# Attention of a two-layer block: when VectorE makes each output's low part, and when it evacuates the first group of an expansion

## Chip, cores and metric

The kernel runs on one core of one Trainium2 chip. The metric is the device time of one execution in microseconds (us), taken as the median of several runs. The engines are TensorE (PE, matmuls), VectorE (DVE), ScalarE (ACT), GpSimd (POOL) and SyncE (SP, which issues the DMAs).

## What is computed

Two transformer-like blocks one after the other, batch 1, 256 positions, model width 1024, all in float32. What matters here are the two attention parts with the projections around them:

```python
# first block: 8 heads of 128; one block of 256 keys, so plain causal attention
p = jax.nn.softmax(jnp.concatenate([s_sel, s_own], axis=-1), axis=-1)
yb = einsum(p_own, v_own)
merged = gates[:, :, 0] * (ya @ w_proj_rnn) + gates[:, :, 1] * (yb @ w_proj_attn)
# second block: 8 sliding-window heads with a sink, then 8 MLA heads
o_a = swa_sink_attention(qa, ka, va, swa_sinks)
q   = (cq @ w_uq);  kvb = ckv @ w_ukv        # the expansions of the latents
o_b = mla_attention(q_nope, q_rope, k_nope, k_rope, vb)
y = sigmoid(g_a) * (o_a @ w_o_swa) + sigmoid(g_b) * (o_b @ w_o_mla)
x = x + y @ w_out
```

The two blocks also have a recurrent branch, RMS norms and feed-forward parts, which the change does not touch.

## The kernel before

**Precision by parts.** Every large product is made of three matmuls on float32r parts: a number is split into a high part (a copy rounded by ScalarE, `whi`, `ahi`) and a low part (the remainder, `number - high`, made by VectorE, `wlo`, `alo`). So every weight tile is read twice before PE may use it.

**Slabs.** The weights come in slabs of 128 x 2048 numbers through a ring of three buffers. For each slab SP loads `raw`, ScalarE makes `whi` (function `hi`, L490, called through `pre`), VectorE makes `wlo` (`lo`, L856, called through `pre`), and PE multiplies. `pre(s + 2)` means that both engines convert the slab that PE uses two slabs later.

**Hand-written order.** Each engine has its own program, written out by hand, loop by loop over the slabs; the only links between engines are semaphores. An engine goes through its own list in that order, and what stands in a list behind a waiting instruction waits too.

**Attention units and steps.** Attention is cut into 24 units: 0 to 7 are the heads of the first block, 8 to 15 the sliding-window heads and 16 to 23 the MLA heads of the second. Each unit goes through a pipeline whose stages are one step apart (`LAG_S` 1, `LAG_E` 2, `LAG_N` 3, `LAG_PT` 4, `LAG_PV` 5), and one call `att(step)` in each engine's program does the engine's share of all stages of that step. In one step PE transposes q and k of a new unit (L1489), multiplies scores of the previous one (L1501, L1502), transposes the probabilities of an older one (L1512) and multiplies the oldest by its values (L1526, L1528; called PV here, and PV(u) for unit u). ScalarE then evacuates: transposes, probabilities (L536), the high part of the PV output (L541), and makes the exponentials (L553). VectorE scales the probabilities (L896 to L898), masks scores and takes maxima (L904 to L915), and makes the **low part** of the PV output (L920), called lo(u) here.

**One PSUM buffer for PV.** `PSPV` is a single bank. lo(u) is the last reader of the output of unit u, and PE asks for it before it overwrites the bank with the next unit (L1518): PV(u) waits for the semaphore `att lo` (`aL`) to count u, which means lo(u-1) has been made. Nothing in PE's list behind PV(u), the matmuls of the slab included, can start before.

**Where the steps stand.** The first block's steps 0 to 12 stand one to a slab: eight gate slabs (G0 to G7 here), four slabs of `w_proj_rnn` (P0 to P3) and the first of `w_proj_attn` (A0). PV(0) is in G5, PV(3) in P0 and PV(7) in A0. The second block's steps 100 to 120 go by `STEPS_AT`: one step each in the slabs of the expansions UQ0, UQ1 and UKV (PV(8), PV(9), PV(10)), two steps each (called A and B here) in GB0 to GB3 and OSWA0, OSWA1 (PV(11) to PV(22)), one in OMLA0 (PV(23)). PE does step A at the start of a slab and step B in its middle (in GB0 a little later).

VectorE's list for such a slab s reads (L1227 to L1260):

```python
for step in steps[:1]: att(step)        # A
pre(s + 2)                              # wlo, behind ScalarE's whi
for step in steps[1:]: att(step)        # B
gate(s, ...)   # or branch(...): evacuation of slab s, needs its last matmul
```

and for one-step slabs `att`, `pre(s + 2)`, then `gate` or `branch`. In UQ0 to UKV `pre(s + 2)` stands at the end of the slab instead (`late_cut`), on ScalarE too. In P3 a second `pre`, that of slab P3 + 3, follows behind `branch` (the `cut()` of L1092). ScalarE's list has `att(A)`, the `whi` of slab s + 2, `att(B)`.

UKV is the slab of `w_ukv`; its four groups of matmuls use two banks in turn. VectorE evacuates groups 0 and 2 (`kv_evac`, L1224), ScalarE groups 1 and 3. PE's group 2 needs the bank of group 0.

Of the kernel before, what the change touches and what calls it, by code (L numbers as in the profile page):

```python
# [17 lines left out]
SEQ = 256  # L18
# [5 lines left out]
HEADS = 8  # L24
# [125 lines left out]
LAG_S, LAG_E, LAG_N, LAG_PT, LAG_PV = 1, 2, 3, 4, 5  # L150


def steps_at(s):

    if S_GATE <= s < S_PR + LAG_PV:
        return [s - S_GATE]
    if S2_GA <= s <= S2_OMLA:
        first = sum(STEPS_AT[:s - S2_GA])
        return [100 + first + i for i in range(STEPS_AT[s - S2_GA])]
    return []  # L160
# [7 lines left out]
def early_att(s):  # L168

    return S_GATE < s < S_PA or S2_GA < s < S2_OUT  # L170


def late_cut(s):

    return S2_UQ <= s <= S2_UKV


def gate_of(s):

    if S2_GA <= s < S2_UQ:  # L180
        return s - S2_GA
    if S2_GB <= s < S2_OSWA:
        return s - S2_GB + S2_UQ - S2_GA
    return None


def unit_of(step):

    if 0 <= step < HEADS:
        return step  # L190
    if 100 <= step < 100 + 2 * HEADS:
        return step - 100 + HEADS
    return None


def program(nc, t):
    f32, f32r = mybir.dt.float32, mybir.dt.float32r
    ALU, ACT, AX = mybir.AluOpType, mybir.ActivationFunctionType, mybir.AxisListType.X
    with ExitStack() as ctx:
        def sb(name, shape, dt=f32):  # L200
            return ctx.enter_context(nc.sbuf_tensor(name, shape, dt))

        def sem(name):
            return ctx.enter_context(nc.semaphore(name))
# [5 lines left out]
        pairs = [(sb(f"ahi{i}", [P, KD, SEQ], f32r), sb(f"alo{i}", [P, KD, SEQ], f32r)) for i in range(2)]  # L210
# [91 lines left out]
        PST, PSS, PSPT, PSPV, PSA, PSB = ps[2], (ps[3], ps[7]), (ps[4], ps[6]), ps[5], ps[6], ps[7]  # L302

        def sums_banks(n):
# [24 lines left out]
        aT, aTe, aS, aM, aE, aN, aPT, aPTe, aPV, aH, aL = (sem(n) for n in (  # L329
            "att_T", "att_T_out", "att_S", "att_max", "att_exp", "att_norm", "att_PT", "att_PT_out",  # L330
            "att_PV", "yb_hi", "yb_lo"))
# [513 lines left out]
        def _(e):  # L845
            count = [0]

            def link(ins):

                count[0] += 1  # L850
                ins.then_inc(dve_step, 1)
                e.wait_ge(dve_step, count[0])
# [6 lines left out]
            def pre(s):  # L859
                if s < SLABS:  # L860
                    lo(s, s % RING)
# [26 lines left out]
            def att(step):  # L888
                kind_base = 0 if step < 100 else 100
                u, un, ul = (unit_of(step - lag) if step - lag >= kind_base else None  # L890
                             for lag in (LAG_S, LAG_N, LAG_PV))
                if un is not None:
                    e.wait_ge(aE, un + 1)
                    if 8 <= un < 16:
                        link(e.tensor_tensor(sums[:, un % 3, :], sums[:, un % 3, :], esink[:, un % 3, :], ALU.add))
                    link(e.reciprocal(rinv[:, un % 2, :], sums[:, un % 3, :]))  # L896
                    e.tensor_scalar(pr[:, un % 3, 0:P], pr[:, un % 3, 0:P], rinv[:, un % 2, 0:1], None, ALU.mult)
                    e.tensor_scalar(pr[:, un % 3, P:3 * P], pr[:, un % 3, P:3 * P], rinv[:, un % 2, 1:2], None,  # L898
                                    ALU.mult).then_inc(aN, 1)
                if u is not None:  # L900
                    e.wait_ge(aS, u + 1)
                    if u >= 2:
                        e.wait_ge(aE, u - 1)
                    link(e.tensor_tensor(sm[:, u % 2, :], PSS[u % 2][:, 0:3 * P],  # L904
                                         masks[:, 1 if 8 <= u < 16 else 0, :], ALU.add))
                    e.reduce_max(mx[:, u % 2, 0:1], sm[:, u % 2, 0:P], AX)
                    link(e.reduce_max(mx[:, u % 2, 1:2], sm[:, u % 2, P:3 * P], AX))
                    if u < 8:
                        e.tensor_tensor(nb[:, u % 3, :], mx[:, u % 2, :], cq[:, 1, :, u], ALU.mult).then_inc(aM, 1)
                    elif u < 16:  # L910
                        hd = swa_head(u)
                        e.tensor_scalar(nb[:, u % 3, :], mx[:, u % 2, :], -(64 ** -0.5), sinks[:, 1, hd:hd + 1],
                                        ALU.mult, ALU.min).then_inc(aM, 1)
                    else:
                        e.tensor_scalar(nb[:, u % 3, :], mx[:, u % 2, :], -(MLA_D ** -0.5), None,  # L915
                                        ALU.mult).then_inc(aM, 1)
                if ul is not None:
                    e.wait_ge(aH, ul + 1)
                    rows, chunk = yb_place(ul)
                    e.tensor_tensor(pairs[2][1][rows, chunk, :], PSPV[rows, 0:SEQ],  # L920
                                    pairs[2][0][rows, chunk, :].bitcast(f32), ALU.subtract).then_inc(aL, 1)


            e.memset(epst[:, :], EPS)
            for b in range(2):
# [112 lines left out]
            def gate(s, i):  # L1038
                normed(GROUP_OF[(s, 0)], gate_tile(i))

            def branch(g, tiles, dst):

                e.wait_ge(group_done, g + 1)
                e.scalar_tensor_tensor(dst[:, tiles, :], dst[:, tiles, :], 1.0,
                                       ps[BANK[g]][:, :].rearrange("p (m n) -> p m n", m=2),
                                       ALU.add, ALU.mult).then_inc(bank_free["dve"], 1)
                e.wait_ge(bank_free["dve"], emptied(g)[1])
# [171 lines left out]
            def kv_evac(i):  # L1219

                g = GROUP_OF[(S2_UKV, i)]
                e.wait_ge(group_done, g + 1)
                for dst, src in kv_parts(ps[BANK[g]], i // 2, 0):
                    ins = e.tensor_copy(dst, src)  # L1224
                ins.then_inc(bank_free["dve"], 1)

            for s in range(S2_GA, FFN2):  # L1227
                steps = steps_at(s)
                if s == S2_UKV:
                    kv_evac(0)  # L1230
                for step in steps[:1]:
                    att(step)
                if early_att(s) and not late_cut(s) and s < S2_OUT - 1:
                    pre(s + 2)
                for step in steps[1:]:
                    att(step)
                if S2_OSWA <= s < S2_OMLA:
                    e.wait_ge(gate_t, 12)
                    c = 4 * (s - S2_OSWA)
                    branch(GROUP_OF[(s, 0)], slice(c, c + 2), T0)  # L1240
                if s == S2_GA + 1:
                    cq_parts(0)
                    cq_parts(1)
                if s == S2_GA + 2:
                    cq_parts(2)
                if gate_of(s) is not None:
                    gate(s, gate_of(s))
                if s == S2_UKV:
                    kv_evac(2)
                if S2_UQ <= s <= S2_UKV:  # L1250
                    pre(s + 2)
                if S2_OSWA <= s < S2_OMLA:
                    c = 4 * (s - S2_OSWA) + 2
                    branch(GROUP_OF[(s, 1)], slice(c, c + 2), T0)
                if S2_OMLA <= s < S2_OUT:
                    e.wait_ge(gate_t, 16)
                    for i in range(2):
                        c = 2 * (s - S2_OMLA) + i
                        branch(GROUP_OF[(s, i)], slice(2 * c, 2 * c + 2), T1)
                        merge(c, 4, (lambda: pre(s + 2)) if s == S2_OUT - 1 and i == 0 else nothing)  # L1260
                if S2_OUT <= s < FFN2:
                    i = s - S2_OUT
                    residual(s, i)
                    if s < FFN2 - 1:
                        pre(s + 3)
                    norm_lo(3, pcol[:, FFNG:FFNG + KD], pairs[2][1], pairs[2][0], (2 * i, 2 * i + 1))
                if s in (S2_OUT - 1, FFN2 - 1):
                    pre(s + 3)
# [455 lines left out]
def swa_head(u):  # L1724

    return (u - 8) // 2 + 4 * ((u - 8) % 2)


def yb_place(u):

    if u < 8:
        return slice(0, P), u
    b = u % 2
    return slice(64 * b, 64 * b + 64), (u - 8) // 2
# [47 lines left out]
```

## Time and profile before

| | |
|---|---|
| median of 3 runs | 825.85 us (825.42 to 826.04) |
| the profiled execution's own time | 825.37 us |
| its span, first to last instruction | 823.5 us |
| PE busy with matmuls | 798.3 us, 97% |
| VectorE busy | 599.6 us, 73% |
| ScalarE busy | 457.7 us, 56% |
| granted TensorE clock, mean | 0.998 |

Busy is the time in which an engine executes; the rest it waits, or has run out of work. The 1.9 us between span and time lie outside the instructions. Of PE's idle time 11.7 us is the start, before the first weights are split.

### The profile page before, as it was taken

The numbers are of one execution on the slowest core, as the hardware profiler recorded it, in microseconds if no ns is written. First come the engines' busy times: TensorE is split into PE (matmuls) and PEld (weight loads), VectorE is DVE, ScalarE is ACT, GpSimd is POOL, SyncE is SP. The second block draws the span as 40 slices with busy tenths as digits, with TensorE's granted clock in tenths as the row PEclk, the third lists the DMA queues.
The fourth block names the chain that finished last, engine by engine and source line by source line (L and its number), as shares of the span: only waits on it lengthen the run. The fifth ranks groups of instructions, "written<-read, shape, count | busy, mean of one in ns | idle before, by whom it ended". The sixth has DMA issues, their size and how long they took to land.

```text
span 823.5 us, 13642 instructions
## 1 busy us (share of the span) xinstructions
PE 798.3 (97%) x5240; PEld 729.5 (89%) x5240; DVE 599.6 (73%) x773; ACT 457.7 (56%) x611; POOL 83.9 (10%) x94
## 2 busy tenths in 40 slices
PE   4999999999999999999999999999999999999996
PEld 4998888999999899999998899889999888888884
DVE  5895798666667898777787868777777856766653
ACT  5669855566335555444444667667556544454443
POOL 2030142000021100000000440500013000000000
PEclk9999999999999999999999999999999999999999
DMA  9997899776878789788886895564669978888841
GB/s 227 218 214 162 189 197 200 159 153 134 174 175 184 156 184 214 166 196 197 179 190 144 183 196 130 106 152 103 134 138 215 202 175 188 197 184 187 193 102 51
DMA packets 112781, 140.99 MB, mean 171 GB/s; under 512 B 5474, under 2 KB 95586, under 8 KB 112738
## 3 DMA queue, kind: packets, MB, share of 16 engines
q1 hardware_dynamic: 112594, 140.30, 78.6%
q8 instruction: 29, 0.48, 0.3%
q14 instruction: 14, 0.11, 0.1%
q10 hardware_dynamic: 144, 0.10, 0.0%
HBM read 139.33 MB, written 1.05 MB: 170 GB/s over the span
## 4 chain that ended last, share of the span: by engine, by line
PE 79%; DVE 10%; ACT 6%; issue 2%; POOL 1%; DMA 1%; SPq 0%; DVEq 0%; ACTq 0%; POOLq 0%
PE pp L1418 20%; PE pp L1377 15%; PE pp L1379 15%; PE pp L1378 15%; PE pp L1420 10%; DVE wlo L856 4%; ACT whi L490 1%; PE pp L1526 1%; POOL vv L1289 1%; PE pp L1502 1%; PE pp L1489 1%; PE pp L1512 1%; DMA raw<-in_w_in 1%; ACT gate L610 1%; PE pp L1501 1%
## 5 line engine op out<-in xcount | busy, mean ns | idle before, releaser
L856 DVE TENSOR_TENSOR wlo<-raw,whi 128x2048 fp32r<-128x2048 f32 x131 | 302.9, 2314 | 123.1 <-ACT whi L490 123.1
L490 ACT ACTIVATE whi<-raw 128x2048 fp32r<-128x2048 f32 x131 | 250.1, 1911 | 98.6 <-PE pp L1379 79.8
L1377 PE MATMUL pp<-ahi,whi 128*128 128x256 f32 x768 | 221.5, 288 | 13.8 <-DVE alo L871 11.7
L1418 PE MATMUL pp<-ahilo,whi 128*128 128x512 f32 x704 | 221.4, 396 | 0.0
L1378 PE MATMUL pp<-alo,whi 128*128 128x256 f32 x768 | 218.5, 284 | 0.0
L1379 PE MATMUL pp<-ahi,wlo 128*128 128x256 f32 x768 | 218.4, 284 | 0.0
L1377 PEld LDWEIGHTS pp<-ahi,whi 128*128 128x128 f32 x768 | 148.5, 193 | 15.5 <-DVE wlo L932 11.7
L1420 PEld LDWEIGHTS pp<-ahilo,wlo 128*128 128x128 f32 x704 | 132.2, 188 | 31.2
L1378 PEld LDWEIGHTS pp<-alo,whi 128*128 128x128 f32 x768 | 148.7, 194 | 0.1
L1379 PEld LDWEIGHTS pp<-ahi,wlo 128*128 128x128 f32 x768 | 148.5, 193 | 0.0
L1420 PE MATMUL pp<-ahilo,wlo 128*128 128x256 f32 x704 | 138.3, 278 | 0.0
L1418 PEld LDWEIGHTS pp<-ahilo,whi 128*128 128x128 f32 x704 | 108.0, 189 | 0.8
L1377 PE MATMUL pp<-whi,ahi 128*128 128x512 f32 (+2 forms) x252 | 97.9, 389 | 1.1 <-DVE alo L1150 1.1
L1379 PE MATMUL pp<-whi,alo 128*128 128x512 f32 (+2 forms) x252 | 96.9, 384 | 0.0
L1378 PE MATMUL pp<-wlo,ahi 128*128 128x512 f32 (+2 forms) x252 | 96.9, 384 | 0.0
L715 ACT ACTIVATE qk<-pp 128x512 f32<-128x512 f32 x44 | 26.3, 598 | 120.0 <-PE pp L1420 120.0
L1108 DVE TENSOR_TENSOR qk<-pp,qk 128x512 f32<-128x512 f32 x44 | 30.4, 690 | 40.9 <-ACT qk L715 40.8
L1377 PEld LDWEIGHTS pp<-whi,ahi 128*128 128x128 f32 x252 | 47.3, 188 | 10.6 <-issue 1.4
L1379 PEld LDWEIGHTS pp<-whi,alo 128*128 128x128 f32 x252 | 47.3, 188 | 9.0
L1378 PEld LDWEIGHTS pp<-wlo,ahi 128*128 128x128 f32 x252 | 47.4, 188 | 8.2
L1289 POOL TENSOR_TENSOR vv<-vv 128x512 f32<-128x512 f32 x12 | 24.1, 2006 | 252.0 <-ACT vv L507 251.5
L1377 PE MATMUL pp<-ahilo,whi 128*128 128x256 f32 x128 | 36.7, 287 | 0.0
(200 smaller groups left out, 847.9 us busy)
## 6 DMA issues: line engine op xcount, KB each, us to landing
raw<-in_w_in SPq DMA_DIRECT2D x80, 512.0 KB, 6.7
raw<-in_w_up SPq DMA_DIRECT2D x44, 512.0 KB, 6.3
raw<-in_w_gate SPq DMA_DIRECT2D x44, 512.0 KB, 6.3
raw<-in_w_down SPq DMA_DIRECT2D x44, 512.0 KB, 6.5
raw<-in_w_out SPq DMA_DIRECT2D x16, 512.0 KB, 6.3
raw<-in_w_proj_rnn SPq DMA_DIRECT2D x8, 512.0 KB, 6.0
raw<-in_w_proj_attn SPq DMA_DIRECT2D x8, 512.0 KB, 6.0
raw<-in_w_o_swa SPq DMA_DIRECT2D x4, 512.0 KB, 5.9
```

The lines of the kernel that those rows point to most:

```text
L490: e.activation(whi[slot][:, :], raw[slot][:, :], ACT.Copy).then_inc(hi_ready, 1)
L610: ins = e.activation(dst, ps[BANK[g]][:, SEQ * m:SEQ * m + SEQ], ACT.Tanh, scale=0.5, bias=halfb[:, 8 * (i // 4) + blk:8 * (i // 4) + blk ...
L715: e.activation(dst, banks[:, :, SEQ:2 * SEQ], ACT.Copy).then_inc(f_cross, 1)
L856: e.tensor_tensor(wlo[slot][:, :], raw[slot][:, :], whi[slot][:, :].bitcast(f32), ALU.subtract).then_inc(lo_ready, 1)
L1108: return e.tensor_tensor(dst, banks[:, :, 0:SEQ], dst, ALU.add)
L1289: e.tensor_tensor(SQ[:, 0:2, :], SQ[:, 0:2, :], SQ[:, 2 * i:2 * i + 2, :], ALU.add).then_inc(folded, 1)
L1377: e.matmul(out, lhs[0], rhs[0], start=first, stop=False, skip_group_check=True)
L1378: e.matmul(out, lhs[0], rhs[1], start=False, stop=False, skip_group_check=True)
L1379: return e.matmul(out, lhs[1], rhs[0], start=False, stop=last, skip_group_check=True)
L1418: e.matmul(out[:, m, :], w[m][0], ACT2[:, k, :], start=k == 0, stop=False, skip_group_check=True)
L1420: ins = e.matmul(out[:, m, 0:SEQ], w[m][1], ACT2[:, k, 0:SEQ], start=False, stop=k == KD - 1, skip_group_check=True)
L1489: ins = e.transpose(PST[0:d, SEQ * i + P * h:SEQ * i + P * h + P], src, ident[:, :])
```

## The change

VectorE's `att(step)` no longer ends with lo(u) of its own PV unit. It begins with the low part of the unit whose PV was in the step before (`unit_of(step - LAG_PV - 1)`). Only the last unit of each block (7 and 23), which has no next step, keeps its low part at the end of its own step. Beside that, `kv_evac(0)` in slab UKV moves from before VectorE's step 107 to behind it. No instruction is added or removed; the lists of PE, ScalarE, GpSimd and SyncE stay as they are.

```diff
--- before.py
+++ after.py
@@ -889,6 +889,9 @@
                 kind_base = 0 if step < 100 else 100
                 u, un, ul = (unit_of(step - lag) if step - lag >= kind_base else None
                              for lag in (LAG_S, LAG_N, LAG_PV))
+                before = unit_of(step - LAG_PV - 1) if step - LAG_PV - 1 >= kind_base else None
+                if before is not None:
+                    out_lo(before)
                 if un is not None:
                     e.wait_ge(aE, un + 1)
                     if 8 <= un < 16:
@@ -914,12 +917,15 @@
                     else:
                         e.tensor_scalar(nb[:, u % 3, :], mx[:, u % 2, :], -(MLA_D ** -0.5), None,
                                         ALU.mult).then_inc(aM, 1)
-                if ul is not None:
-                    e.wait_ge(aH, ul + 1)
-                    rows, chunk = yb_place(ul)
-                    e.tensor_tensor(pairs[2][1][rows, chunk, :], PSPV[rows, 0:SEQ],
-                                    pairs[2][0][rows, chunk, :].bitcast(f32), ALU.subtract).then_inc(aL, 1)
-
+                if ul is not None and ul in (7, 8 + 2 * HEADS - 1):
+                    out_lo(ul)
+
+            def out_lo(u):
+
+                e.wait_ge(aH, u + 1)
+                rows, chunk = yb_place(u)
+                e.tensor_tensor(pairs[2][1][rows, chunk, :], PSPV[rows, 0:SEQ],
+                                pairs[2][0][rows, chunk, :].bitcast(f32), ALU.subtract).then_inc(aL, 1)
 
             e.memset(epst[:, :], EPS)
             for b in range(2):
@@ -1226,10 +1232,10 @@
 
             for s in range(S2_GA, FFN2):
                 steps = steps_at(s)
+                for step in steps[:1]:
+                    att(step)
                 if s == S2_UKV:
                     kv_evac(0)
-                for step in steps[:1]:
-                    att(step)
                 if early_att(s) and not late_cut(s) and s < S2_OUT - 1:
                     pre(s + 2)
                 for step in steps[1:]:
```

**Place 1: VectorE in a slab with two steps (GB2, MLA units).** The rows before run from the low part of step A to the low part of step B and the gate (`gate<-pp`) behind it; L920 is the low part, L856 the `wlo` of the slab two ahead.

```order
L920 TENSOR_TENSOR ahilo<-pp,ahilo 64x256
L856 TENSOR_TENSOR wlo<-raw,whi 128x2048
L896 RECIPROCAL rinv<-sums 128x2
L897 TENSOR_SCALAR pr<-pr,rinv 128x128
L898 TENSOR_SCALAR pr<-pr,rinv 128x256
L904 TENSOR_TENSOR sm<-pp,masks 128x384
L906 TENSOR_REDUCE mx<-sm 128x1
L907 TENSOR_REDUCE mx<-sm 128x1
L915 TENSOR_SCALAR nb<-mx 128x2
L920 TENSOR_TENSOR ahilo<-pp,ahilo 64x256
L885 TENSOR_TENSOR gate<-pp,rstd_bc 128x512
```

The same stretch of the changed program, where L927 is the low part:

```order
L856 TENSOR_TENSOR wlo<-raw,whi 128x2048
L927 TENSOR_TENSOR ahilo<-pp,ahilo 64x256
L899 RECIPROCAL rinv<-sums 128x2
L900 TENSOR_SCALAR pr<-pr,rinv 128x128
L901 TENSOR_SCALAR pr<-pr,rinv 128x256
L907 TENSOR_TENSOR sm<-pp,masks 128x384
L909 TENSOR_REDUCE mx<-sm 128x1
L910 TENSOR_REDUCE mx<-sm 128x1
L918 TENSOR_SCALAR nb<-mx 128x2
L885 TENSOR_TENSOR gate<-pp,rstd_bc 128x512
L927 TENSOR_TENSOR ahilo<-pp,ahilo 64x256
```

The low part of step A stood ahead of `wlo` and stands behind it; that of step B stood ahead of the gate and stands behind it.

**Place 2: VectorE from slab P2 to slab A0 of the first block.** L1044 (L1050 in the changed program) is `branch`, the evacuation of a slab. Before:

```order
L856 TENSOR_TENSOR wlo<-raw,whi 128x2048
L1044 SCALAR_TENSOR_TENSOR gate<-gate,pp 128x512
L920 TENSOR_TENSOR ahilo<-pp,ahilo 128x256
L856 TENSOR_TENSOR wlo<-raw,whi 128x2048
L1044 SCALAR_TENSOR_TENSOR gate<-gate,pp 128x512
L856 TENSOR_TENSOR wlo<-raw,whi 128x2048
L920 TENSOR_TENSOR ahilo<-pp,ahilo 128x256
L1044 SCALAR_TENSOR_TENSOR gate<-gate,pp 128x512
```

And now:

```order
L856 TENSOR_TENSOR wlo<-raw,whi 128x2048
L1050 SCALAR_TENSOR_TENSOR gate<-gate,pp 128x512
L927 TENSOR_TENSOR ahilo<-pp,ahilo 128x256
L856 TENSOR_TENSOR wlo<-raw,whi 128x2048
L1050 SCALAR_TENSOR_TENSOR gate<-gate,pp 128x512
L856 TENSOR_TENSOR wlo<-raw,whi 128x2048
L927 TENSOR_TENSOR ahilo<-pp,ahilo 128x256 x2
L1050 SCALAR_TENSOR_TENSOR gate<-gate,pp 128x512
```

The low part of unit 6 was in front of two `wlo` and a `branch`; it is now behind them, next to that of unit 7.

**Place 3: VectorE from the end of slab UQ1 to GB0.** L1224 (L1230 in the changed program) is `kv_evac`, two copies for each group. Before:

```order
L920 TENSOR_TENSOR ahilo<-pp,ahilo 64x256
L856 TENSOR_TENSOR wlo<-raw,whi 128x2048
L1224 COPY gg<-pp 128x4x64
L1224 COPY qk<-pp 128x256
L895 TENSOR_TENSOR sums<-sums,esink 128x2
...
L912 TENSOR_SCALAR nb<-mx,sinks 128x2
L920 TENSOR_TENSOR ahilo<-pp,ahilo 64x256
L1224 COPY gg<-pp 128x4x64
L1224 COPY qk<-pp 128x256
L856 TENSOR_TENSOR wlo<-raw,whi 128x2048
```

And now:

```order
L856 TENSOR_TENSOR wlo<-raw,whi 128x2048
L927 TENSOR_TENSOR ahilo<-pp,ahilo 64x256
L898 TENSOR_TENSOR sums<-sums,esink 128x2
...
L915 TENSOR_SCALAR nb<-mx,sinks 128x2
L1230 COPY gg<-pp 128x4x64
L1230 COPY qk<-pp 128x256
L1230 COPY gg<-pp 128x4x64
L1230 COPY qk<-pp 128x256
L856 TENSOR_TENSOR wlo<-raw,whi 128x2048
L927 TENSOR_TENSOR ahilo<-pp,ahilo 64x256
```

The first two copies moved behind the step's arithmetic, and both low parts moved behind the `wlo` that followed them.

## Rows read from the trace of the kernel before

**Rows 1.** The page, busy time of PE over the whole span
```profile
PE 798.3 (97%) x5240; PEld 729.5 (89%) x5240; DVE 599.6 (73%) x773; ACT 457.7 (56%) x611; POOL 83.9 (10%) x94
```

**Rows 2.** Who PE waited for, whole span: us, times, longest
```profile
PE pp L1526 <- DVE ahilo L920: 1.2, 2, 0.7
...
PE pp L1377 <- DVE qk L1224: 0.4, 1, 0.4
```

**Rows 3.** Timeline, UKV: start us, us, engine, instruction, [idle before it]
```profile
530.24 0.43 DVE L920 TENSOR_TENSOR ahilo<-pp,ahilo 64x256 fp32r<-64x256 f32 x1
...
530.82 0.67 PE L1526 MATMUL pp<-pT,qk 128*128 128x256 f32 x2 [0.46 <-DVE ahilo L920]
```

**Rows 4.** Timeline, slab OSWA0, PE, ACT and DVE
```profile
578.69 0.39 PE L1501 MATMUL pp<-qkT 96*128 96x128 f32 x2
...
579.68 0.60 PE L1526 MATMUL pp<-pT,qk 128*128 128x256 f32 x2
...
581.62 0.43 DVE L920 TENSOR_TENSOR ahilo<-pp,ahilo 64x256 fp32r<-64x256 f32 x1
581.83 1.90 ACT L490 ACTIVATE whi<-raw 128x2048 fp32r<-128x2048 f32 x1
...
583.53 0.60 PE L1526 MATMUL pp<-pT,qk 128*128 128x256 f32 x2
583.76 2.29 DVE L856 TENSOR_TENSOR wlo<-raw,whi 128x2048 fp32r<-128x2048 f32 x1 [1.71 <-ACT whi L490]
...
585.97 0.16 DVE L896 RECIPROCAL rinv<-sums 128x2 f32<-128x2 f32 x1
```

**Rows 5.** Timeline, slab GB2
```profile
560.31 0.60 PE L1526 MATMUL pp<-pT,qk 128*128 128x256 f32 x2
...
565.27 0.60 PE L1526 MATMUL pp<-pT,qk 128*128 128x256 f32 x2
...
566.60 0.16 DVE L896 RECIPROCAL rinv<-sums 128x2 f32<-128x2 f32 x1
```

**Rows 6.** Timeline, slabs UQ0 to UKV
```profile
524.65 0.60 PE L1526 MATMUL pp<-pT,qk 128*128 128x256 f32 x2
...
525.41 2.43 DVE L856 TENSOR_TENSOR wlo<-raw,whi 128x2048 fp32r<-128x2048 f32 x1 [4.22 <-ACT whi L490]
...
531.10 2.44 DVE L856 TENSOR_TENSOR wlo<-raw,whi 128x2048 fp32r<-128x2048 f32 x1 [0.43 <-ACT whi L490]
```

**Rows 7.** Timeline, slab GB0
```profile
541.02 0.60 PE L1526 MATMUL pp<-pT,qk 128*128 128x256 f32 x2
...
542.13 0.15 DVE L895 TENSOR_TENSOR sums<-sums,esink 128x2 f32<-128x2 f32 x1
...
545.25 0.60 PE L1526 MATMUL pp<-pT,qk 128*128 128x256 f32 x2
...
547.50 0.15 DVE L895 TENSOR_TENSOR sums<-sums,esink 128x2 f32<-128x2 f32 x1
```

**Rows 8.** Timeline, start of slab P3 (w_proj_rnn)
```profile
214.98 0.49 PE L1512 MATMUL pp<-ident,pr 128*128 128x128 f32 x3
...
215.25 0.69 DVE L1044 SCALAR_TENSOR_TENSOR gate<-gate,pp 128x512 f32<-128x512 f32 x1 [1.31 <-PE pp L1379]
215.30 0.60 PE L1526 MATMUL pp<-pT,vv 128*128 128x256 f32 x2
```

**Rows 9.** Timeline, start of slab A0 (w_proj_attn)
```profile
221.71 0.60 PE L1526 MATMUL pp<-pT,vv 128*128 128x256 f32 x2
...
226.19 0.42 DVE L920 TENSOR_TENSOR ahilo<-pp,ahilo 128x256 fp32r<-128x256 f32 x1
```

**Rows 10.** Stretches: busy by engine (instructions), granted PE clock, DMA, GB/s
```profile
12.00:18.00 6.00, 6.00 (x30) 6.00 (x30) 5.97 (x11) 5.74 (x10) 2.84 (x3) 1.00 1.12 222
170.00:226.00 56.00, 56.00 (x455) 55.19 (x454) 36.38 (x58) 29.75 (x53) 0.00 (x0) 1.00 0.69 150
817.00:821.00 4.00, 0.00 (x0) 0.00 (x0) 3.15 (x6) 2.07 (x7) 0.00 (x0) 0.87 0.35 131
```


## The prediction

> **What bounds the kernel now.** I read the page first, then PE's waits, then the timeline of both attention parts. The page has PE busy for 97% of the span [rows 1], so what matters is whether the change adds to PE's waits or takes some away. There is little to take: over the whole span PE waited 1.2 us for a low part, twice, and 0.4 us for the evacuation of the expansion [rows 2]. VectorE and ScalarE look idle a third of the time, but in the attention they are on a leash: `wlo` starts when `whi` ends, `whi` starts when ScalarE has done step A, and step A contains the evacuation of PV(A). What the reader is to see in the rows of slab OSWA0 [rows 4] is how close behind PE that loop runs.
>
> **The price list.** Where PE was caught waiting for a low part, PV started 530.82 - 530.24 = 0.58 us after the low part's start [rows 3]. I use 0.57 throughout. After such a wait PE loses about 0.07 us more (PV's pair takes 0.67 instead of 0.60 us [rows 3, 4]).
>
> **Step B of the two-step slabs.** PV(B) needs lo(A). Before, lo(A) stood ahead of `wlo`; in OSWA0 it began at 581.62, and PV(B) at 583.53 found it done 1.5 us earlier [rows 4]. Now it stands behind `wlo` (place 1). `whi` runs from 581.83 to 583.73, `wlo` from 583.76, and the instruction behind it begins at 585.97 [rows 4]. That is where lo(A) goes, so PV(B) starts at 585.97 + 0.57 = 586.54, 3.0 us late. Can `wlo` come earlier? No: `whi` follows PV(A) by 2.15 us and all of that is ScalarE's step A, so the loop moves with PE and the loss comes back in each slab. The same sum for the others:
> - GB2: 566.60 + 0.57 - 565.27 = 1.9 us [rows 5]. GB1 and GB3 have the same pattern at 1.9 us each, so 5.7 in all.
> - GB0: 547.50 + 0.57 - 545.25 = 2.8 us [rows 7].
> - OSWA0: 3.0 us. OSWA1 has less arithmetic in its step; between the 1.9 of GB2 and the 3.0 of OSWA0 I take 2.1.
>
> Together 13.6 us.
>
> **The one-step slabs of the expansions.** `wlo` stands at the end of the slab here, and the low part behind it.
> - PV(9) needs lo(8), which goes behind the `wlo` of 525.41. That one takes 2.43 us, and the next instruction overlaps its end by some 0.08, so 527.76 + 0.57 = 528.33 against 524.65: 3.7 us [rows 6].
> - PV(10) needs lo(9), behind the `wlo` of 531.10. If nothing had moved: 531.10 + 2.36 + 0.57 = 534.03, against an arrival of 530.82 - 0.46 = 530.36 [rows 3, 6], 3.7 us. PE's arrival and `whi`, which waits for UQ1's last group, both move by the 3.7 us of PV(9); ScalarE gains back some 0.2 us of backlog (an estimate). I take 3.5, and 3.0 net of the old wait of 0.46.
> - PV(11) needs lo(10), behind the `wlo` that ends before 542.13: 542.13 + 0.57 - 541.02 = 1.7 us [rows 7]. In this slab two small waits for `kv_evac` fall away (next part), 0.4 us each; the first moves PE and `whi` together, the second only PE, which makes the wait 2.0 and the net loss 1.3.
> - PV(13) had the wait of 0.7 us [rows 2]; its lo(12) has only the gate in front of it now, and PE comes to it later by all the waits above, so it is in time (next part): -0.7.
>
> Together 7.3 us.
>
> **Behind the evacuation of a slab.** Ahead of PV(1) to PV(6) and of PV(13), (15), (17), (19), (21) and (23) the low part goes behind `gate` or `branch`, which needs the last matmul of the slab before. `branch` begins 0.27 us after PE's first instruction of the new slab (215.25 - 214.98 [rows 8]), takes 0.69 and waits for its own end (0.72, an estimate), then 0.57: PV may start 1.56 us into the slab. In P3 it started at 0.32 [rows 8], so 1.2 us each for PV(4), PV(5), PV(6) and PV(21), 4.9 us, and 1.5 us for PV(23), which is PE's first instruction. `gate` has no wait for its own end, and the next instruction overlaps it by some 0.08 as behind `wlo` (585.97 against 583.76 + 2.29 [rows 4]): 0.60 us, 1.44 in all. With scores but no transposes ahead PV comes at 0.99 us (579.68 - 578.69 [rows 4]), 0.45 each for PV(3) and PV(19); with transposes, four instructions more, it comes at about 1.4, and I cost PV(2), (13), (15) and (17) at nothing. What covers them is just that arithmetic of PE; were it gone, each would cost 1.1. PV(1) finds VectorE 0.6 us behind: 0.6. Together 7.9 us. VectorE's own step starts 0.4 us later everywhere; behind it stands only scaling and masking, which waits for ScalarE's `whi` afterwards in any case.
>
> **Unit 6, the worst one.** PV(7) in A0 needs lo(6). Before, that was made in P3's step. Now it stands behind `wlo`, `branch`, and the second `wlo` (place 2), in the place where lo(7) began at 226.19: 226.19 + 0.57 - 221.71 = 5.05 us [rows 9].
>
> **`kv_evac(0)`.** It moves behind step 107, some 2.1 us. Had PE not been held up, that would be 2 us on PE's group 2. But PV(10) stands ahead of group 0 and now waits, so VectorE has finished its step (2.5 us behind the start of lo(9)) when group 0 ends, and the evacuation of 0.75 us ends before PE wants group 2, about 3.2 us behind PV(10). Cost nothing; this cover is PE's own new wait. The two old waits go, 0.4 us as in [rows 2], and as much, an estimate, for GB0's first group, which waits for the other evacuation.
>
> **The sum.** 13.6 + 7.3 + 7.9 + 5.05 = 33.9 us, and 15 restarts of 0.07 us make 1.0: 34.9 us. PE has no slack to give it back. Against the profiled execution's 825.37 us that is 860.3; the median of the runs lies 0.5 us above it, so I predict 860.5 us.
>
> **TensorE's clock.** At the start of the program PE does 30 matmuls in 6 us, where the attention stretch has 455 in 56 us, 49 in 6 [rows 10]. The granted clock reads 1.00 in both, but the spacing of the first is that of the lower of the two levels, 1.2 GHz. The slow spell cost some 19 / 8.1 = 2.3 us. Near the end, in 4 us without a matmul, the mean granted clock is 0.87 [rows 10], so it fell to the lower level in the last microsecond of them. The new wait before PV(7) is longer than that, those before PV(9) and PV(10) about as long.
>
> The Trainium skill says the same (TensorE: Matmul & The Clock Gate, "HAM oscillation — how this bites in real kernels"): an idle gap puts the clock back to its lower level, and the next stretch of work starts slow. By that rule the sum would be three such spells longer; the gap at the end agrees, and no gap inside this kernel was long enough to show it.
>
> **Rivals.**
> - *The clock falls at all three long waits*: 860.5 + 3 x 2.3 = 867.4 us. For it: the fall near the end. Against it: two of the three waits are only as long as the gap after which the row shows the fall. One fall, at PV(7), gives 862.8 and counts to the forecast.
> - *The loop doesn't move with PE*: once PE is late, `whi` and `wlo` run on ahead, only the first wait of each kind is paid. Then about half, 17 us: 843. For it: ScalarE is busy 56%. Against it: `whi` begins right behind ScalarE's step A [rows 4].
> - *Faster*: VectorE is held up by lo(u) waiting for ScalarE's high part, and the change frees it. The three known waits of PE, 0.46, 0.7 and 0.4 us, go: 825.85 - 1.6 = 824.2 us. That needs lo(A) done by the time of PV(B), which is to say 585.97 + 0.57 before 583.53; it misses by 3 us.
> - *No change*: if the two orders made VectorE reach lo(A) at the same time as before. In every two-step slab a whole `wlo` of 2.3 us lies between the places.
>
> **How the numbers follow.** Forecast, 853 to 865 us: 0.66. Clock, 865 to 872: 0.12. The loop catches up, 835 to 853: 0.16. Faster 0.03, no change 0.01, beyond these 0.02. The range that leaves out no more than two in ten reaches into both neighbours: 848 to 868. A difference of 0.2% or less is about what a measurement of this kernel can't tell from none. Faster 0.03, same 0.01, slower 0.96.
>
> **What the changed profile would show.** Right: PE's waits for L927 about 15 to 18 times, 35 us together; the longest, 5 us, at the first `w_proj_attn` slab; in each two-step slab PV(B) 0.57 us behind the start of a low part that stands directly behind `wlo`; no wait for `kv_evac`. PE's busy share falls to 93%. Wrong in size: two-step slabs whose PV(B) waits less than 1 us (the loop caught up), or slow matmuls behind PV(7). Wrong altogether: PE's waits for the low part at 2 us or less.

## The result and the profile after

The changed kernel takes 872.43 us (median of 4 runs, 871.56 to 876.26), the kernel before 825.63 us in the same session: a ratio of 1.0575, 95% interval 1.0555 to 1.0595, 46.8 us more. The profiled execution took 871.61 us, its span is 869.8 us and its mean granted TensorE clock 0.980 where it was 0.998. The prediction was 860.5 us in a range of 848 to 868, so the direction and the waits were right and the time lies above the range.

The page of the changed kernel, PE's busy time and the granted clock in 40 slices of the span (tenths, 9 is 90% or more):

```profile
PE 813.7 (94%) x5240; PEld 741.5 (85%) x5240; DVE 600.4 (69%) x773; ACT 457.5 (53%) x611; POOL 81.8 (9%) x94
...
PEclk9999999999999999999999998799899999999999
```

With the same 5240 matmuls PE is busy for 15.4 us longer than in [rows 1], which waits alone can't do (a restart behind each adds some 0.07 us, 1.3 us in all). That is the first sign of something beside waits: matmuls that got slower. Slices 25, 26 and 29 of the span (522 to 565 and 609 to 631 us), in the second block's attention, show where it is most.

PE's waits, total us, times, longest:

```profile
PE pp L1532 <- DVE ahilo L927: 33.0, 18, 4.9
```

Against 1.2 us in [rows 2]: 31.8 us more, in 18 places. PE no longer waits for the evacuation of the expansion.

The timeline of the changed kernel at A0, UQ1, UKV and OSWA0 (start, us, engine, instruction, idle before it); L927 is the low part, L1532 PV:

```profile
228.64 2.29 DVE L856 TENSOR_TENSOR wlo<-raw,whi 128x2048 fp32r<-128x2048 f32 x1 [1.31 <-ACT whi L490]
230.85 0.42 DVE L927 TENSOR_TENSOR ahilo<-pp,ahilo 128x256 fp32r<-128x256 f32 x1
231.41 0.92 PE L1532 MATMUL pp<-pT,vv 128*128 128x256 f32 x2 [4.88 <-DVE ahilo L927]
...
539.62 1.19 PE L1532 MATMUL pp<-pT,qk 128*128 128x256 f32 x2 [3.49 <-DVE ahilo L927]
...
551.85 1.19 PE L1532 MATMUL pp<-pT,qk 128*128 128x256 f32 x2 [4.04 <-DVE ahilo L927]
...
615.94 0.46 PE L1532 MATMUL pp<-pT,qk 128*128 128x256 f32 x1 [0.21 <-DVE ahilo L927]
...
618.17 1.89 ACT L490 ACTIVATE whi<-raw 128x2048 fp32r<-128x2048 f32 x1
...
620.10 2.29 DVE L856 TENSOR_TENSOR wlo<-raw,whi 128x2048 fp32r<-128x2048 f32 x1 [2.33 <-ACT whi L490]
...
622.42 0.43 DVE L927 TENSOR_TENSOR ahilo<-pp,ahilo 64x256 fp32r<-64x256 f32 x1
...
622.99 0.67 PE L1532 MATMUL pp<-pT,qk 128*128 128x256 f32 x2 [2.96 <-DVE ahilo L927]
```

OSWA0 is the loop of [rows 4] with the low part behind `wlo`: PV(A) at 615.94, `whi` 2.23 us later, `wlo`, the low part, and PV(B) 0.57 us behind its start, 2.96 us late. PV(7) in A0 waits 4.88 us.

Stretches of the changed kernel (busy by engine and instructions, then granted clock):

```profile
232.00:235.00 3.00, 3.00 (x15) 2.91 (x15) 0.43 (x1) 0.38 (x1) 0.00 (x0) 0.50 0.87 211
552.00:555.00 3.00, 3.00 (x9) 2.43 (x10) 2.05 (x7) 1.44 (x6) 0.00 (x0) 0.50 0.76 169
596.00:597.00 1.00, 1.00 (x7) 0.95 (x8) 0.93 (x4) 0.09 (x1) 0.00 (x0) 0.96 0.91 31
597.00:600.00 3.00, 3.00 (x16) 3.00 (x16) 0.99 (x4) 1.69 (x6) 0.00 (x0) 0.50 0.83 197
```

This is the missing part. At 0.50 of the granted clock, the lower level of 1.2 GHz, PE starts 5 matmuls in a microsecond in the first and the last row instead of the 8 of [rows 10] (3 in the second row, where most are 512 columns wide). Read microsecond by microsecond, there are seven such stretches: behind PV(7), around PV(9) and around PV(10), and four in the two-step slabs, behind the waits ahead of PV(11), PV(16), PV(18) and PV(20). The last two rows show the least expected thing: the wait ahead of PV(16) was only 1.87 us long and ended at 595.98; the clock fell a microsecond later, with PE busy, and stayed low for more than 3 us. The wait ahead of PV(14), as long, had no such stretch behind it.

### The profile page after: what moved, and what is told of

It is laid out like the page before. It is cut to its first block, busy times and chain, and to the rows that moved or that the text cites. A ratio compares the mean times of both kernels' runs of the same rounds, so it can differ in the third digit from the quotient of the medians.

```text
span 869.8 us, 13642 instructions
## 1 busy us (share of the span) xinstructions
PE 813.7 (94%) x5240; PEld 741.5 (85%) x5240; DVE 600.4 (69%) x773; ACT 457.5 (53%) x611; POOL 81.8 (9%) x94
## 4 chain that ended last, share of the span: by engine, by line
PE 71%; DVE 14%; ACT 10%; issue 3%; POOL 1%; DMA 1%; DVEq 0%; SPq 0%; ACTq 0%; POOLq 0%
PE pp L1424 19%; PE pp L1383 13%; PE pp L1384 13%; PE pp L1385 13%; PE pp L1426 9%; DVE wlo L856 7%; ACT whi L490 4%; PE pp L1532 2%; POOL vv L1295 1%; ACT pr L553 1%; DVE ahilo L927 1%; DMA raw<-in_w_in 1%; ACT gate L610 1%; PE pp L1534 1%; DVE gate L885 1%
## 5 line engine op out<-in xcount | busy, mean ns | idle before, releaser
L856 DVE TENSOR_TENSOR wlo<-raw,whi 128x2048 fp32r<-128x2048 f32 x131 | 302.7, 2313 | 143.6 <-ACT whi L490 143.5
L1383 PEld LDWEIGHTS pp<-ahi,whi 128*128 128x128 f32 x768 | 150.5, 196 | 14.8 <-DVE wlo L938 11.5
L1384 PEld LDWEIGHTS pp<-alo,whi 128*128 128x128 f32 x768 | 150.7, 196 | 0.1
L1385 PEld LDWEIGHTS pp<-ahi,wlo 128*128 128x128 f32 x768 | 150.5, 196 | 0.0
```

Source lines behind the costliest of these rows:

```text
L856: e.tensor_tensor(wlo[slot][:, :], raw[slot][:, :], whi[slot][:, :].bitcast(f32), ALU.subtract).then_inc(lo_ready, 1)
L1383: e.matmul(out, lhs[0], rhs[0], start=first, stop=False, skip_group_check=True)
L1384: e.matmul(out, lhs[0], rhs[1], start=False, stop=False, skip_group_check=True)
L1385: return e.matmul(out, lhs[1], rhs[0], start=False, stop=last, skip_group_check=True)
```

## Experiments

The theory after the result: PE's waits for late low parts cost the predicted 35 us; what is beyond that is matmuls at the lower clock, brought about by the same waits. The rivals: the low clock has another cause; the evacuation that moved costs part of it; VectorE's later list hurts at other places than PV. The experiments ran in three sessions, in which the kernel before had medians of 826.27, 826.05 and 826.00 us; in that of the changed kernel it had 825.63. Where a run is compared with the changed kernel's 872.43, up to 0.6 us of the difference is between sessions.

**Only the first block** (`e1_first_block`): the changed kernel with the low parts of units 8 to 23 and the evacuation back as before (`...` stands for lines left out, here those of the evacuation too).

```diff
+OWN = (7, *range(8, 24))
...
-                if before is not None:
+                if before is not None and before not in OWN:
                     out_lo(before)
...
-                if ul is not None and ul in (7, 8 + 2 * HEADS - 1):
+                if ul is not None and ul in OWN:
                     out_lo(ul)
...
```

> Late low parts in the first block alone (units 0 to 6); units 8 to 23 and the first evacuation of the expansion as before. Theory (PE's waits for the low part plus the slow matmuls that follow the long ones): the first block's share, 9.7 us of delay up to PV(7) and 2.3 us of slow matmuls behind it, so 825.6 + 12 = 838 us, and one stretch of low clock. Rival (the low clock comes on its own, the waits are only half of it): the first block has no low clock in it and 835 us or less, or several stretches and over 841.

Measured 837.36 us (836.50 to 837.99), ratio 1.0134 (1.0117 to 1.0151). Its PE waits for low parts:

```profile
PE pp L1533 <- DVE ahilo L928: 9.9, 8, 4.9
```

and one stretch at the lower clock, between 233 and 237 us. So the first block's share is 11.1 us, which leaves about 36 for the second.

**Only the evacuation** (`e2_kv_only`): the kernel before with `kv_evac(0)` behind step 107.

```diff
-                if s == S2_UKV:
-                    kv_evac(0)
                 for step in steps[:1]:
                     att(step)
+                if s == S2_UKV:
+                    kv_evac(0)
```

> Only the first evacuation of the expansion is moved behind VectorE's step, all low parts as before. Theory (its cover is PE's new wait ahead of PV(10), which is gone here): PE's third group in the slab waits some 2 us for the evacuation, 0.4 before, so 827 to 828 us. Rival (a free move, or a gain, since the step starts earlier): 824.5 to 825.6 us.

Measured 829.10 us (828.56 to 831.44), ratio 1.0047 (1.0028 to 1.0066): 2.8 us more, a little above what was expected. Its PE waits for the expansion's evacuation (total us, times, longest, as in all rows of waits):

```profile
PE pp L1377 <- DVE qk L1224: 2.7, 1, 2.7
```

The wait grew from the 0.4 us of [rows 2] to 2.7. The move is not free in itself; in the changed kernel PE's wait ahead of PV(10) covers it. No low stretch follows this wait of 2.7 us: the only ones in this profile are at the start and the end of the program.

**The waits filled with work** (`e8_filled`): the changed kernel, in which PE multiplies by a zero tile instead of standing idle. `out` is the bank of the slab in hand, `FILL` has the number of matmuls that fit into each unit's wait. The tile `zero` is set to 0 at the start.

```diff
+FILL = {1: 3, 3: 1, 4: 8, 5: 8, 6: 8, 7: 40, 9: 28, 10: 27, 11: 16, 12: 22, 14: 15, 16: 15, 18: 15, 20: 24, 21: 8, 22: 16, 23: 11}
...
+        zero = sb("zero", [P, MLA_D], f32r)
...
                 u = unit_of(step - LAG_PV) if step - LAG_PV >= kind_base else None
                 if u is not None:
                     e.wait_ge(aPTe, u + 1)
+                    for _ in range(FILL.get(u, 0)):
+                        e.matmul(out[0:MLA_D, 0:SEQ], zero[:, :], ACT0[:, 1, :], start=False, stop=False,
+                                 skip_group_check=True)
                     if u >= 1:
                         e.wait_ge(aL, u)
```

> The changed kernel, with extra matmuls of a zero stationary tile (96 columns wide, 256 moving columns, 0.12 us each) in PE's list in front of each wait for a low part, as many as fit into that wait (257 in all); they add zeros to the slab's own bank. PE is busy where it used to wait. Theory (the low clock is a consequence of PE's idle gaps and costs some 11 us on top of the 35 of the waits): granted clock 1.00, no slow matmuls, 860 to 862 us. Rival (the low clock is not due to the gaps, or the waits themselves are what costs all 47 us): clock 0.98 and 871 us or more.

Measured 861.41 us (860.28 to 862.50), ratio 1.0430 (1.0411 to 1.0449). (The text on record says 257 matmuls; the list has 265.) What is left of PE's waits for low parts:

```profile
PE pp L1540 <- DVE ahilo L929: 1.2, 4, 0.7
```

Stretches, busy by engine, then the granted clock; first two of the filled kernel, a piece of its start and nearly all the rest:

```profile
22.00:24.00 2.00, 2.00 (x10) 2.00 (x11) 1.43 (x1) 1.97 (x3) 0.00 (x0) 0.50 1.12 206
26.00:821.00 795.00, 790.14 (x5281) 723.99 (x5280) 566.02 (x732) 428.38 (x567) 79.10 (x86) 1.00 0.78 167
```

and of the changed kernel, most of the second block's attention:

```profile
560.00:645.00 85.00, 68.33 (x473) 64.30 (x472) 47.17 (x102) 42.49 (x89) 0.00 (x0) 0.92 0.41 87
```

The order of VectorE's list is exactly that of the changed kernel, the low parts stand just as late in it, and 11.0 us are gone because PE is hardly ever idle there. So the lower clock in the attention is a consequence of the gaps and costs 11 us; the waits by themselves cost 861.41 - 826.27 = 35.1 us. The sum had 34.9. The stretch of low clock at 22 us lies ahead of all that was filled; the last section comes back to it. Free of the start are the times from PV(0) to PV(23) in the three profiles: 422.7 us before (172.04 to 594.76), 457.4 filled (173.02 to 630.37) and 469.4 in the changed kernel (171.62 to 640.98). That makes 34.6 us for the waits and 12.0 for the clock.

**Which gaps bring the clock down.** `e10_filled_long` fills only those ahead of PV(7), PV(9) and PV(10), `e11_filled_short` all but these.

```diff
+FILL = {7: 40, 9: 28, 10: 27}
```

> As the filled kernel, but only the three long waits are filled with zero matmuls, those ahead of PV(7), PV(9) and PV(10) (95 of them). Theory (each long idle gap brings its own stretch of low clock: 2.3 us of work lost behind PV(7), 3.0 behind PV(9), 2.1 behind PV(10)): 872.4 - 7.4 = 865 us, and low clock left only in the two-step slabs. Rival (the long gaps start it and the short ones inherit it): no low clock at all and 861 us.

> The complement: all the waits but those three are filled (the gaps of 0.2 to 3 us, 170 zero matmuls). Theory (gaps of 1.9 to 3 us, one in each two-step slab, bring stretches of low clock too; in the changed kernel's profile they cost 4 x 1.75 us of work, less 1.5 us that the shorter wait ahead of PV(12) gave back): 872.4 - 5 = 867 us, and low clock left only behind the three long waits. Rival (only the long gaps count, the slow stretches in the two-step slabs follow from them): they stay in the trace as busy but slow matmuls, and 871 us or more.

Filling the long ones gives 866.99 us (863.38 to 869.49), filling the short ones 867.55 us (866.62 to 869.22). Against 872.43 that is 5.4 and 4.9 us, together 10.3 of the 11.0 of filling all; the first kernel's runs lie 6 us apart, so the two shares are rough. Stretches with the long ones filled (busy by engine, then the granted clock):

```profile
225.00:240.00 15.00, 14.84 (x124) 14.56 (x123) 5.41 (x8) 4.28 (x4) 0.00 (x0) 1.00 0.65 141
535.00:557.00 22.00, 20.79 (x131) 17.93 (x129) 12.30 (x25) 11.44 (x26) 8.26 (x14) 1.00 0.47 95
589.00:594.00 5.00, 4.30 (x21) 4.15 (x22) 2.58 (x9) 1.77 (x6) 0.00 (x0) 0.66 0.59 146
```

and with the short ones filled:

```profile
225.00:240.00 15.00, 10.12 (x65) 9.77 (x64) 5.22 (x5) 2.29 (x2) 0.00 (x0) 0.77 0.68 141
560.00:640.00 80.00, 79.12 (x610) 74.62 (x609) 47.20 (x103) 41.86 (x89) 0.00 (x0) 1.00 0.43 93
```

The two halves don't touch each other: in the attention the clock stays up where the gaps are filled, and low stretches stand only where they are not. With the long ones filled the two-step slabs have five (the changed kernel's profile had four), behind the waits ahead of PV(11), PV(16), PV(18), PV(20) and PV(22). So gaps of 1.9 to 3 us bring the clock down too, and cost about as much together as the three long ones. The 170 matmuls named in the text on record for the second kernel are 170 in its list as well.

**The low parts of step A back ahead of `wlo`** (`e7_a_units_own`): as the first experiment, with `OWN = (7, 11, 13, 15, 17, 19, 21, 23)` on the changed kernel.

> The changed kernel with the low parts of units 11, 13, 15, 17, 19 and 21 (step A of the two-step slabs) back at the end of their own step, ahead of wlo. Theory (a wlo between VectorE's old and new place is what PE waits for): their waits of 2.1, 1.9, 1.9, 1.9, 3.0 and 1.3 us go, and with them the four stretches of slow matmuls of these slabs at some 1.9 us each, so 872.4 - 12 - 7 = 853 us, with three stretches of low clock left (behind PV(7), PV(9), PV(10)). Rival 1 (gaps shorter than 2 us do nothing to the clock, its stretches there come from the two long waits ahead): 860 us. Rival 2 (VectorE stays late anyway and PE waits at step A instead): over 866 us.

Measured 855.36 us (854.53 to 855.71), ratio 1.0354 (1.0336 to 1.0371): 17.1 us less than the changed kernel where 19 were expected. Its PE waits for low parts:

```profile
PE pp L1533 <- DVE ahilo L928: 22.4, 13, 4.9
```

and the stretch of its second block's attention, busy by engine, then the granted clock:

```profile
560.00:640.00 80.00, 73.79 (x577) 70.70 (x576) 56.77 (x113) 46.63 (x95) 2.94 (x2) 1.00 0.50 108
```

The clock is at its upper level from there on. Rival 1, that the low stretches there are an echo of the long waits, would have left them: the long waits and the low stretches around them are all still in this profile. The wait of 2.09 us ahead of PV(11) is unchanged too, and here no low stretch follows it. The waits fell by 10.6 us instead of 12: two of the waits at step A are longer here (PV(13) 1.30 us where there was none, PV(21) 1.21 instead of 1.07), since PE is no longer late.

**Unit 6 alone back** (`e6_unit6_own`, `OWN = (6, 7, 23)`).

> The changed kernel with the low part of unit 6 back at the end of its own step. Theory (that one place costs 4.9 us of waiting and the one stretch of slow matmuls of the first block, 2.3 us): 872.4 - 7.2 = 865.2 us, and no low clock before the second block. Rival (the wait is only moved to the neighbours): over 869 us.

Measured 866.70 us (864.64 to 870.13), ratio 1.0481 (1.0460 to 1.0502): 5.7 us less, where 7.2 were expected; the theory's 865.2 lies inside the spread. The low stretch of the first block is gone, and PE waits for low parts 3.3 us less in all, the 4.88 us ahead of PV(7) gone and the others together 1.6 us longer. Nearly all of that is PV(12), the second row:

```profile
PE pp L1533 <- DVE ahilo L928: 29.7, 17, 4.1
...
568.05 0.67 PE L1533 MATMUL pp<-pT,qk 128*128 128x256 f32 x2 [2.78 <-DVE ahilo L928]
```

In this execution no slow matmuls follow the wait ahead of PV(11), so PE comes to PV(12) early and waits 2.78 us for it; in the changed kernel's profile it came late and waited 1.26.

The profiled execution (870.13 us) was the slowest of the four. It has one more low stretch in the second block than the changed kernel's, and one at the start of the program, which that had not.

**Two banks for PV** (`e4_two_banks`): VectorE's list as in the changed kernel, but PE asks for the low part before last. The second bank is one of the two that the transposed probabilities had; they now share one, and PE waits for its evacuation before each new unit's transposes.

```diff
-        PST, PSS, PSPT, PSPV, PSA, PSB = ps[2], (ps[3], ps[7]), (ps[4], ps[6]), ps[5], ps[6], ps[7]
+        PST, PSS, PSPT, PSPV, PSA, PSB = ps[2], (ps[3], ps[7]), (ps[4], ps[4]), (ps[5], ps[6]), ps[6], ps[7]
...
-                    if u >= 2:
-                        e.wait_ge(aPTe, u - 1)
+                    if u >= 1:
+                        e.wait_ge(aPTe, u)
...
-                    if u >= 1:
-                        e.wait_ge(aL, u)
+                    if u >= 2:
+                        e.wait_ge(aL, u - 1)
...
-                    e.matmul(PSPV[:, 0:SEQ], v[0], pT[:, u % 2, 0:SEQ], start=True, stop=False,
+                    e.matmul(PSPV[u % 2][:, 0:SEQ], v[0], pT[:, u % 2, 0:SEQ], start=True, stop=False,
...
```

> The changed kernel with two PSUM banks for PV's output in turn (the probabilities' transposes share one bank in exchange), so PV(u) needs the low part of unit u-2 and no longer that of u-1; the order of VectorE's list is that of the changed kernel. Theory (the one bank hands VectorE's delay to PE): the waits for low parts go to under 1 us, the clock stays at 1.00, and 2 us stay for the evacuation of the expansion, whose cover is gone: 826 to 827.5 us. Rival (VectorE's list itself is late, for the norms and scores too): PE waits at its transposes and scores instead, over 835 us.

Measured 830.45 us (829.75 to 831.02), ratio 1.0051 (1.0034 to 1.0068). No wait for a low part is left, all 33 us are gone, so the single bank is what hands VectorE's delay to PE. But the time is 3 us above what was expected. Of its PE waits in the attention this one grew most, for the evacuation of the expansion:

```profile
PE pp L1383 <- DVE qk L1230: 3.7, 1, 3.7
```

and around it stands this stretch, busy by engine, then the granted clock, 0.50:

```profile
538.00:543.00 5.00, 4.46 (x11) 3.49 (x12) 1.25 (x4) 0.00 (x0) 0.00 (x0) 0.50 0.66 128
```

The evacuation, without its cover, now has PE wait 3.7 us, and slow matmuls follow. That is 1 us more than with the evacuation alone moved, most of it because PV(10) no longer waits and PE comes 0.7 us sooner. **With the evacuation back in front** (`e9_two_banks_kv_first`) this can be told apart.

> The changed kernel with two banks for PV's output and the first evacuation of the expansion back in front of VectorE's step. Theory (late low parts cost nothing once PE does not ask for them, and of the run with two banks all its excess was the evacuation: 3.7 us of wait and the slow matmuls behind it): 824.3 us, or 1.2 to 1.5 us less than before, no low clock inside the program. Rival (late low parts have a price of their own, norms and scores starting 0.4 us later): 826 us or more.

Measured 826.11 us (824.59 to 829.71, 12 runs), ratio 0.9999 (0.9986 to 1.0011). All 46.8 us are undone with VectorE's low parts still one step late. It is not the gain that was expected, and the time lies in the rival's range: the waits for the evacuation are 1.1 us where they were 0.4, and a wait of 0.3 for scaled probabilities is new, which together eat most of the 1.2 us gained. In the profiled run the clock was low at the start of the program as well. Its PE waits for these two:

```profile
PE pp L1383 <- DVE qk L1230: 1.1, 2, 0.7
...
PE pp L1518 <- DVE pr L901: 0.3, 1, 0.3
```

**The kernel before with two banks** (`e5_before_two_banks`).

> The kernel before with two PSUM banks for PV's output in turn (low parts and evacuation where they were before). Theory (PE's two waits for a low part, 0.46 and 0.7 us, are all that one bank costs there): 1.2 us less, 824.4 us where before is 825.6, and no PE wait for a low part. Rival (the shared bank of the transposes costs as much, or ScalarE sets the pace anyway): 825.3 us or more.

Measured 825.34 us (823.89 to 826.33, 12 runs), ratio 0.9989 (0.9980 to 0.9998). It is 0.7 us faster than the kernel before, barely outside the noise, where 1.2 were expected: the 1.2 us of waiting for low parts went, and the waits for the evacuation, which PE reaches earlier, grew from 0.4 to 1.0. The run before this one differs only in its late low parts and took 0.8 us more; whether they still cost that is not clear of the noise. Its PE waits for the evacuation:

```profile
PE pp L1377 <- DVE qk L1224: 1.0, 2, 0.6
```

## Why the prediction was right in the waits and wrong in the time

- **Step B of the two-step slabs, 13.6 us.** Right. Measured 1.87, 1.87, 1.86, 2.96 and 2.08 us for units 14, 16, 18, 20 and 22, where 1.9, 1.9, 1.9, 3.0 and 2.1 stood. Unit 12 waited 1.26 instead of 2.8, because PE arrived late after slow matmuls; without these, in `e6_unit6_own`, it waited 2.78. The loop does move with PE: the rival in which it catches up, 843 us, would have shown shrinking waits.
- **The one-step slabs.** Right for PV(9), 3.49 us against 3.7, and PV(11), 2.09 against 2.0; PV(10) waited 4.04 instead of 3.5.
- **Behind `gate` and `branch`, 7.9 us, and PV(7), 5.05.** Right in place, somewhat too high in size. PV(4) to PV(6) and PV(21) waited 1.07 us each against 1.2, PV(23) 1.39 against 1.5, PV(1) 0.45 against 0.6, PV(3) and PV(19) 0.2 against 0.45: 6.5 us in all instead of 7.9. PV(7) waited 4.88.
- **The sum of the waits.** 34.9 us with their restarts; with PE kept busy in them 35.1 were measured. That it fits so closely is in part luck: the 1.4 us too much behind `gate` and `branch` are made up for by 0.5 too little at PV(10), by three more waits with a restart than the 15 counted, and probably by the low clock at the start of the filled kernel's runs.
- **`kv_evac(0)` at nothing.** Right, and right about its cover: alone it costs 2.8 us where "2 us" stood, and with two banks, where PV(10) doesn't wait at all, PE waits 3.7 us for it.
- **The step that failed: TensorE's clock.** The sum stood at 34.9 us with the clock left out ("Against the profiled execution's 825.37 us that is 860.3"), and the rival *the clock falls at all three long waits* had 0.12 and stopped at 3 x 2.3 us. Measured are seven stretches and 11 us. The sum priced each wait at its own length and put the slow matmuls behind it at nothing. Two things were mis-sized. I gave a stretch only to waits as long as the idle time after which the end of the program shows a fall [rows 10]; waits of 1.9 to 3 us bring it down as well (they cost 4.9 us, the long ones 5.4 where the rival had 6.9). And I took even the long ones as the exception. The rule of the Trainium skill that stood beside it (TensorE: Matmul & The Clock Gate, "HAM oscillation — how this bites in real kernels") was the better guide in kind: a kernel whose PE waits again and again in the same place starts again and again at the lower clock. The seven stretches agree. The waits in the page's example are 3 to 5 us long, though, like the three long ones here; for waits of 1.9 to 3 us it is the runs of this case that show it.
- **The rivals on the other side**, faster and no change, fell with the first look at the waits.

What stays open: which of the short gaps bring the clock down. Length does not decide it: the wait of 2.7 us in `e2_kv_only` had no low stretch behind it, nor had the 2.09 us ahead of PV(11) in two of the profiles, and 1.87 us were enough elsewhere. In the changed kernel's profile the wait ahead of PV(14), 1.87 us, had no low stretch behind it and that ahead of PV(16), as long, had one. The four runs of the kernel lie between 871.56 and 876.26 us with mean clocks of 0.977 to 0.983, so it differs from run to run.

## What to carry to other kernels

An instruction that frees a buffer for the bound engine belongs in front of the long, off-path work of its own engine, however cheap it is: 0.4 us of VectorE moved behind a `wlo` of 2.3 us cost PE 1.9 to 3 us in most of the two-step slabs. When an order shift makes the bound engine wait regularly, price the waits from the timeline (here the sum came out within 1%, the single waits mostly within 0.25 us and at worst 1.5 us off), and then price the clock too, for short gaps as well as long. If the order can't be helped, a second buffer takes the delay away (826.11 us against 826.05 before).

## What the runs showed of the hardware that was not expected

- A wait of 1.87 us was followed, 1 us after it ended and with PE busy, by more than 3 us at the lower clock (0.50), 5 matmuls a microsecond instead of 8.
- Multiplying by zeros in the gaps keeps the granted clock at 1.00 from 26 to 821 us and saves 11.0 of 872.4 us, although it does nothing for the result and moves no low part forward in VectorE's list.
- The start of the program has a low stretch of 3 to 7 us in some executions and not in others. Of the twelve profiles the five in which PE got through 38 or more matmuls from 12 to 18 us (`e2_kv_only`, `e4_two_banks`, `e8_filled`, `e9_two_banks_kv_first`, `e11_filled_short`) all have it at 22 to 24 us, of the seven with 36 or fewer only one (`e6_unit6_own`). In the profile of `e9_two_banks_kv_first`, with 41, PE then waited 0.98 us for GpSimd and 1.00 us for VectorE just there; the kernel before, with 30, waited once, 0.84 us. What decides it is open: in `e1_first_block`, with 28, PE waited 1.91 us for GpSimd there and the clock stayed up. Seven further executions of the kernel before lie between 824.77 and 826.99 us at mean clocks of 0.998 down to 0.995, which fits such a stretch in some of them.
